# Wide moving operand in the upward matmuls of two MLPs: high and low tokens side by side, two PSUM banks a piece

## What is computed

```python
def rms_norm(x, g):
    xf = x.astype(jnp.float32)
    y = xf * lax.rsqrt(jnp.mean(xf * xf, axis=-1, keepdims=True) + EPS)
    return (y * g.astype(jnp.float32)).astype(x.dtype)

def sq_relu_mlp(h, w_up, w_down):          # w_up 1024 x 4096, w_down 4096 x 1024
    return jnp.square(jax.nn.relu(h @ w_up)) @ w_down

for layer in range(2):
    x = x + mix(layer, rms_norm(x, norm_mix_g[layer]))
    x = x + sq_relu_mlp(rms_norm(x, norm_mlp_g[layer]), mlp_w_up[layer], mlp_w_down[layer])
```

## Time and profile before

| | us |
|---|---|
| median of 3 runs (lowest, highest) | 897.57 (897.37, 898.06) |
| the profiled execution | 897.22 |
| its span, from first to last instruction | 895.4 |
| TensorE busy in the span | 887.2 (99%) |
| VectorE busy | 572.0 (64%) |
| ScalarE busy | 466.5 (52%) |
| DMA: mean rate | 184 GB/s |

### The profile page before, as it was taken

One profiled execution on the slowest core, in us unless ns is written; L12 is line 12 of the kernel. 1 busy time (PEld: TensorE's weight loads), 2 busy tenths in 40 slices (PEclk: granted clock), 3 DMA queues, 4 the chain that ended last, 5 costly groups with the idle time before them and its releaser, 6 DMA issues.

```text
span 895.4 us, 14765 instructions
## 1 busy us (share of the span) xinstructions
PE 887.2 (99%) x5978; PEld 787.2 (88%) x5978; DVE 572.0 (64%) x948; ACT 466.5 (52%) x747; POOL 59.7 (7%) x69
## 2 busy tenths in 40 slices
PE   9999999999999999999999999999999999999998
PEld 5998799999997888669999999878898889999996
DVE  5769675555554395566556565564567798888764
ACT  5686454444443387646555544454367674344550
POOL 0010000000000045400000000031100000000000
PEclk9999999999999999999999999999999999999999
DMA  8625786555545745378555555530535455554541
GB/s 303 256 94 188 272 316 223 202 187 188 188 143 179 280 146 184 131 259 325 187 197 191 183 188 188 188 106 1 188 111 186 143 186 179 181 183 145 184 144 47
DMA packets 30885, 164.99 MB, mean 184 GB/s; under 512 B 3425, under 2 KB 9953, under 8 KB 12514
## 3 DMA queue, kind: packets, MB, share of 16 engines
q1 hardware_dynamic: 30818, 164.04, 51.6%
HBM read 162.98 MB, written 1.05 MB: 183 GB/s over the span
## 4 chain that ended last, share of the span: by engine, by line
PE 93%; DVE 3%; ACT 1%; DMA 1%; issue 1%; POOL 0%; DVEq 0%; SPq 0%; POOLq 0%; ACTq 0%
PE ps L283 15%; PE ps L285 15%; PE ps L284 15%; PE ps L296 11%; PE ps L297 11%; PE ps L298 11%; PE ps L424 2%; PE ps L361 1%; PE ps L926 1%; PE ps L925 1%; PE ps L924 1%; DMA BI<-in_dbias_dram 1%; DVE WL L1592 1%; PE ps L839 1%; PE ps L864 1%
## 5 line engine op out<-in xcount | busy, mean ns | idle before, releaser
L1592 DVE TENSOR_TENSOR WL<-RAW,WH 128x1024 fp32r<-128x1024 f32 (+1 forms) x260 | 307.1, 1218 | 109.9 <-ACT WH L1002 109.5
L283 PE MATMUL ps<-XAh,WH 128*128 128x256 f32 x1152 | 330.1, 287 | 0.0
L285 PE MATMUL ps<-XAh,WL 128*128 128x256 f32 x1152 | 325.9, 283 | 0.0
L284 PE MATMUL ps<-XAl,WH 128*128 128x256 f32 x1152 | 325.9, 283 | 0.0
L1002 ACT CAST WH<-RAW 128x1024 fp32r<-128x1024 f32 (+1 forms) x264 | 262.1, 1044 | 64.7 <-PE ps L298 62.0
L283 PEld LDWEIGHTS ps<-XAh,WH 128*128 128x128 f32 x1152 | 220.8, 192 | 9.1 <-issue 6.6
L284 PEld LDWEIGHTS ps<-XAl,WH 128*128 128x128 f32 x1152 | 220.8, 192 | 1.8 <-issue 0.7
L285 PEld LDWEIGHTS ps<-XAh,WL 128*128 128x128 f32 x1152 | 220.8, 192 | 0.0
L296 PE MATMUL ps<-WH,HTh 128*128 128x512 f32 x256 | 99.9, 390 | 0.0
L297 PE MATMUL ps<-WL,HTh 128*128 128x512 f32 x256 | 99.9, 390 | 0.0
L298 PE MATMUL ps<-WH,HTl 128*128 128x512 f32 x256 | 99.6, 389 | 0.0
(11 more groups left out here) (258 smaller groups left out, 1101.5 us busy)
## 6 DMA issues: line engine op xcount, KB each, us to landing
RAW<-in_w_dram SPq DMA_DIRECT2D x141, 1024.0 KB, 5.0
RI<-in_w_dram SPq DMA_DIRECT2D x2, 1024.0 KB, 10.6
GB<-in_gb_dram SPq DMA_DIRECT2D x4, 512.0 KB, 6.7
BI<-in_dbias_dram SPq DMA_DIRECT2D x16, 128.0 KB, 4.7
NB<-in_nbias_dram SPq DMA_DIRECT2D x16, 128.0 KB, 2.6
RAW<-in_w_dram SPq DMA_DIRECT2D x2, 528.0 KB, 3.6
X<-in_x_dram SPq DMA_DIRECT2D x4, 256.0 KB, 3.5
RAW<-in_w_dram SPq DMA_DIRECT2D x2, 512.0 KB, 6.6
```

The lines of the kernel that those rows point to most:

```text
L283: T.e.matmul(dst, h, xh[:, k, :], start=k == 0, stop=False)
L284: T.e.matmul(dst, h, xl[:, k, :], start=False, stop=False)
L285: last = T.e.matmul(dst, l, xh[:, k, :], start=False, stop=k == 7)
L1592: D.e.tensor_tensor(M.WL[:, c.s, sl], M.RAW[:, c.r, sl], M.WH[:, c.s, sl].bitcast(F32), ALU.subtract).then_inc(*S.lo.tick(key, a))
```

## The change

- The two XA tiles become halves of one tile X2 (128 x 8 x 512): for each k, 256 high token columns and 256 low ones side by side.
- A new routine `columns_wide` makes the upward pieces 2 to 15 of both MLPs. For each m and k there are two matmuls: high weights by all 512 columns of X2, into a whole bank, and low weights by the 256 high columns, into that bank's first half. So a piece takes two banks: even pieces 4 and 5, odd ones 6 and 7.
- ScalarE copies the second halves of the two banks into RL, without relu; VectorE adds the first halves from PSUM (new semaphore `up`) and then makes max(r, 0) * r into SQ. Pieces 0 and 1 keep the old way out, and their square takes the new form as well.
- TensorE waits for `up` of piece j-2 where it waited for the relu, at piece 2 for the relu of piece 1, at piece 3 for HTh and HTl of piece 0 (MLP 1: the ada columns too).
- In MLP 1 the context transposes go between upward piece j and downward piece j-2 of the rounds 6 and 10, behind a wait for `up` of j-1; the shift on ScalarE comes right after the copy of the rounds 6 and 10, ahead of the weight casts; pieces 7 and 11 wait for it.
- Later users of banks 4 to 7 wait for `up`.

```diff
--- before.py
+++ after.py
@@ -139,7 +139,9 @@
 
         self.WH = self.tile("WH", [128, NW, 2048], F32R)
         self.WL = self.tile("WL", [128, NW, 2048], F32R)
-        self.XA = self.tile("XAh", [128, 8, 256], F32R), self.tile("XAl", [128, 8, 256], F32R)
+        self.X2 = self.tile("XA", [128, 8, 512], F32R)
+        self.XA = self.X2[:, :, 0:256], self.X2[:, :, 256:512]
         at = self.top
         self.XB = self.tile("XBh", [128, 8, 256], F32R), self.tile("XBl", [128, 8, 256], F32R)
         self.top = at
@@ -226,7 +228,8 @@
         self.top = tmp
         self.CV2 = self.tile("CV2", [128, 2, 512])
         self.YB, self.YC = ([v[:, 4 * z:4 * z + 4, :] for v in self.XB] for z in range(2))
-        self.PS = [stack.enter_context(nc.psum_tensor(f"ps{i}", [128, 512], F32)) for i in range(8)]
+        self.banks = stack.enter_context(nc.psum_tensor("ps", [128, 8, 512], F32))
+        self.PS = [self.banks[:, i, :] for i in range(8)]
         self.stats, self.columns_used = {}, 0
         self.CH = chunks()
         self.ORDER = [key for key, _ in order() if self.CH[key].i is not None]
@@ -283,6 +286,20 @@
             T.e.matmul(dst, h, xh[:, k, :], start=k == 0, stop=False)
             T.e.matmul(dst, h, xl[:, k, :], start=False, stop=False)
             last = T.e.matmul(dst, l, xh[:, k, :], start=False, stop=k == 7)
+    return last
+def columns_wide(T, M, S, key, bank):
+    c = M.CH[key]
+    for m, a in ((0, 0), (0, 1), (1, 0), (1, 1)):
+        T.wait_ge(*S.hi.at(key, a))
+        T.wait_ge(*S.lo.at(key, a))
+        for k in range(4 * a, 4 * a + 4):
+            h, l = weights_of(M, c, k * 256 + m * 128, 128)
+            T.e.matmul(M.PS[bank + m][:, :], h, M.X2[:, k, :], start=k == 0, stop=False)
+            last = T.e.matmul(M.PS[bank + m][:, 0:256], l, M.XA[0][:, k, :], start=False, stop=k == 7)
     return last
 
 
@@ -516,16 +533,28 @@
         T.wait_ge(*S.htl.at(l, j))
 
     for j in range(2, 16):
-        T.wait_ge(*S.relu.at(l, j - 2))
-        columns_matmul(T, M, S, ("up", l, j), M.XA, 4 + j % 2).then_inc(*S.freed.tick("up", l, j))
+        if j == 2:
+            T.wait_ge(*S.relu.at(l, 1))
+        elif j == 3:
+            T.wait_ge(*S.hth.at(l, 0))
+            T.wait_ge(*S.htl.at(l, 0))
+            if l:
+                T.wait_ge(*S.adac.at(2))
+        else:
+            T.wait_ge(*S.up.at(l, j - 2))
+        if l and j in (7, 11):
+            for n in range(2):
+                T.wait_ge(*S.cev.at(j // 4 - 1, n))
+        columns_wide(T, M, S, ("up", l, j), 4 + 2 * (j % 2)).then_inc(*S.freed.tick("up", l, j))
+        if l and j in (6, 10):
+            context_transposes(T, M, S, j // 4 - 1, j)
         hready(j - 2)
         for t, n in TN:
             if j == 2:
                 T.wait_ge(*S.res.at("dsa" if l else "rec", t, n))
             made = rows_group(T, M, S, ("down", l, j - 2), hidden(j - 2), 0, t, n, j == 2, False)
         made.then_inc(*S.freed.tick("down", l, j - 2))
-        if l and j in (5, 9):
-            context_transposes(T, M, S, j // 4 - 1)
 
     for t in range(2):
         for n in range(2):
@@ -538,14 +567,11 @@
                     made.then_inc(*S.acc.tick(f"mlp{l}", t, n))
 
 
-def context_transposes(T, M, S, t):
+def context_transposes(T, M, S, t, j):
+    T.wait_ge(*S.up.at(1, j - 1))
     for n in range(2):
         T.wait_ge(*S.cxn.at(t, n))
-        if t == 0:
-            T.wait_ge(*(S.htl.at(1, 0) if n else S.adac.at(2)))
-        else:
-            T.wait_ge(*S.cev.at(0, n))
         for q in range(4):
             at = n * 512 + q * 128
             made = T.e.transpose(M.PS[6 + n][:, q * 128:(q + 1) * 128], M.CX[:, at:at + 128], M.cc("id", 0, 128))
@@ -559,8 +585,7 @@
 
 def tensor_dsa(T, M, S):
     k = 2
-    T.wait_ge(*S.relu.at(0, 15))
-    T.wait_ge(*S.htl.at(0, 0))
+    T.wait_ge(*S.up.at(0, 15))
     ada_matmul(T, M, S, 1, 0, 5)
     norm_transposes(T, M, S, k, 0)
     ada_matmul(T, M, S, 1, 1, 5)
@@ -579,7 +604,6 @@
         if not t:
             made.then_inc(*S.kv.tick())
 
-    T.wait_ge(*S.relu.at(0, 14))
     ckv(0, 4)
     norm_transposes(T, M, S, k, 1)
     ada_matmul(T, M, S, 1, 2, 5)
@@ -747,8 +771,7 @@
 
 def tensor_second(T, M, S):
     free = {b: S.res.at("mlp1", b // 2, b % 2) for b in range(4)}
-    free[4], free[5] = S.relu.at(1, 14), S.relu.at(1, 15)
-    free[6], free[7] = S.cev.at(1, 0), S.cev.at(1, 1)
+    free[4], free[5], free[6], free[7] = S.up.at(1, 14), S.up.at(1, 14), S.up.at(1, 15), S.up.at(1, 15)
 
     def take(b):
         T.wait_ge(*free[b])
@@ -1139,14 +1162,17 @@
     def relu(j):
         A.wait_ge(*S.freed.at("up", l, j))
         if j >= 2:
-            A.wait_ge(*S.htl.at(l, j - 2))
-        elif j == 0:
+            A.wait_ge(*S.sq.at(l, j - 2))
+            b = 4 + 2 * (j % 2)
+            A.e.copy(M.RL[:, j % 2, :].rearrange("p (m q) -> p m q", m=2), M.banks[:, b:b + 2, 256:512]).then_inc(*S.relu.tick(l, j))
+            return
+        if j == 0:
 
             if l:
                 A.wait_ge(*S.pv.at(7))
             else:
                 A.wait_ge(*S.ybl.at(3))
-        A.e.activation(M.RL[:, j % 2, :], M.PS[4 + j % 2 if j else 4][:, :], AF.Relu).then_inc(*S.relu.tick(l, j))
+        A.e.activation(M.RL[:, j, :], M.PS[4 + j][:, :], AF.Relu).then_inc(*S.relu.tick(l, j))
 
     def hth(j):
         if j:
@@ -1180,6 +1206,8 @@
     high(A, M, S, "down", l, 1)
     for j in range(2, 16):
         relu(j)
+        if l and j in (6, 10):
+            context_shift(j // 4 - 1)
         if j < 14:
             high(A, M, S, "up", l, j + 2)
         if j == 14:
@@ -1187,8 +1215,6 @@
         hth(j)
         if l and j in (4, 8):
             context_squares(j // 4 - 1)
-        if l and j in (6, 10):
-            context_shift(j // 4 - 1)
         if j < 14:
             high(A, M, S, "down", l, j)
         if j == 14:
@@ -1827,9 +1853,14 @@
         D.wait_ge(*S.relu.at(l, j))
         if j >= 2:
             D.wait_ge(*S.hth.at(l, j - 2))
+            b = 4 + 2 * (j % 2)
+            r = M.RL[:, j % 2, :].rearrange("p (m q) -> p m q", m=2)
+            D.e.tensor_tensor(r, M.banks[:, b:b + 2, 0:256], r, ALU.add).then_inc(*S.up.tick(l, j))
+            D.wait_ge(*S.up.at(l, j))
         elif j == 0 and l == 0:
             D.wait_ge(*S.ybh.at(3))
-        D.e.tensor_tensor(M.SQ[:, j % 2, :], M.RL[:, j % 2, :], M.RL[:, j % 2, :], ALU.mult).then_inc(*S.sq.tick(l, j))
+        D.e.scalar_tensor_tensor(out=M.SQ[:, j % 2, :], in0=M.RL[:, j % 2, :], scalar=0.0, in1=M.RL[:, j % 2, :],
+                                 op0=ALU.max, op1=ALU.mult).then_inc(*S.sq.tick(l, j))
 
     def hidden_low(j):
         D.wait_ge(*S.hth.at(l, j))
@@ -2647,6 +2678,7 @@
     S.arow = count("arow", [0, 1, 2])
     hidden = [(l, j) for l in layers for j in range(16)]
     S.relu, S.hth = count("relu", hidden), count("hth", hidden)
+    S.up = count("up", [(l, j) for l, j in hidden if j > 1])
     S.cev, S.fev = count("cev", TN), count("fev", TN)
     S.kc, S.qiev = count("keys", range(2)), count("queries", range(2))
     S.kiev = then(S.kc, range(2))
```

## The result

| | before | changed | ratio, 95% interval |
|---|---|---|---|
| median of 7 runs each, us | 897.78 | 894.45 | 0.9958 (0.9947 to 0.9968) |
| the same pair in a second comparison | 898.19 | 893.66 | 0.9952 (0.9939 to 0.9966) |
| span of the profiled execution | 895.4 | 893.0 | |

The time fell by 3.3 us, and by 4.5 in the second comparison. 892.1 was forecast from 897.57, 5.5 us less. The size is that of rival (a), 895.1: its loops were to give 3.0 - 0.5 = 2.5 us, and they gave 2.6. The rest came from outside the loops.

What follows compares the result with a forecast made beforehand. TensorE's spacing of matmul starts was taken to bound the MLP loops. 897.22 profiled - 5.97 (pair) + 0.5 (wait at piece 2) = 891.75; the median is 0.35 above: 892.1 us, range 891.0 to 896.0.

Steps and rivals of the forecast that it cites:

- rival (a): Upward pieces: each wide and narrow pair pays part of the size switch, 0.0067 us; 895.1 us in all; chance 0.13.
- wrong if the pair is not 0.347: Sign set beforehand: TensorE steps inside a late upward piece should take 0.347 us, else the prediction is wrong.
- The pair: Upward pieces 2 to 15, both MLPs: three 256-column matmuls become one of 512 and one of 256; 5.97 us saved.
- I take no surcharge: Upward pieces: surcharge and refund of adjacent size switches were taken to offset each other, leaving 0.3467 us a step.
- The middle value: Upward pieces: a pair pays a third of the first step's surcharge, 0.0067 us; 3.0 us saved.
- The fixed part: TensorE in the MLP loops: each matmul costs 0.0133 us beyond its columns, which dropping 448 matmuls saves.
- Rival (b): MLP loops: the apparent 13.3 ns per matmul mostly comes from unlike neighbours; about 1.1 us saved, 897.0 us; chance 0.08.
- whatever its size: TensorE: the 0.0133 us beyond the columns was claimed for every matmul width, from a line through 256 and 512 columns.
- The wait at piece 2: TensorE waits until ScalarE has read piece 1 from bank 5: 0.5 us stall in MLP 0, nothing in MLP 1.
- The way out: ScalarE copy, VectorE add and new square after upward pieces: some 22 us more VectorE work, hidden, costing nothing.
- The context tiles: MLP 1: moved transposes, shift and second tile's DMA cost nothing, with slacks of 2.4 us and 6 us.
- The gain should reach the end: After the MLPs: a chain through TensorE starts earlier by as much as the loops save, so the whole gain arrives.

Runs made afterwards that it cites:

- runs of 16: Changed kernel with all 16 wide matmuls of a piece first, then its 16 narrow ones: 890.66 us beside 898.52 of the kernel before, ratio 0.9912.
- 2 and 2: Changed kernel with two wide, then two narrow matmuls by turns: 890.95 us, run once.
- 4 and 4: Changed kernel with four wide, then four narrow matmuls in each group of four contraction steps: 893.06 us, run once.

## Why the prediction was right and wrong

The range held the time, and the direction was right. But by its own sign ("wrong if the pair is not 0.347") the prediction was wrong about its main term: the pair took 0.353. The loops alone would have given 897.57 - 2.6 = 895.0, which is inside the range because the range was drawn to hold rival (a). That the measured 894.45 lies nearer to the forecast than this is luck: it comes from a stretch that was not in the sum.

- **The pair**, forecast 5.97 us: pieces of 5.64 instead of 5.75, 26 x 0.112 and 0.19 in the two first pieces, 3.1 us. The step that failed is "I take no surcharge". The surcharge after a change of size was in the rows (0.70 and 0.69), and I let its refund on the way back cancel it. In strict alternation the wide matmul keeps paying 6 to 14 ns and the narrow one returns 0 to 7. The middle value, 0.0067 a pair, would have been right (0.0058 over a piece, 0.0066 inside): rival (a). My reason against it, that the surcharge belongs to a run's start, should have counted for it: in this change every wide matmul starts a run.
- **The fixed part** of 13.3 ns is real for both sizes: in runs of 16 the starts are 0.2263 and 0.120 again. Rival (b) is refuted at its root. The Trainium skill ("TensorE: Matmul & The Clock Gate", section "Wait — 56ns, not 53.3ns?") has 2.5 ns for this term; in these matmuls, each with a weight load of its own, it is 13.3. But "whatever its size" is wrong: at 128 columns the weight load sets the distance (0.112).
- **The wait at piece 2**, forecast 0.5: idle 0.49 in MLP 0, none in MLP 1.
- **The way out**: hidden, as forecast. The square in its new form costs what the old one did (691 ns in both kernels, where up to 0.75 us was allowed), and VectorE's busy time rose by 17.5 us, not 20 to 24. In MLP 0, between 124 and 269 us, TensorE is busy 145.00 of 145.00.
- **The context tiles**: the numbers came close to those worked out. Rows of ScalarE, TensorE and SP's waits in the changed kernel, the end of piece 6 at 461.97:

```profile
462.65 2.91 ACT L1228 ACTIVATE TB<-ps,ADA,AB 128x128 f32<-128x128 f32 x8
...
468.30 0.39 PE L301 MATMUL ps<-XA,WH 128*128 128x512 f32 x1
...
469.56 2.00 ACT L1025 CAST WH<-RAW 128x1024 fp32r<-128x1024 f32 x2 [3.99 <-DMA RAW<-in_w_dram]
...
SPq L127 <- PE ps L577: 18.3, 1, 18.3
```

  The shift ends at T + 3.6 (3.9 was worked out), before piece 7 at T + 6.3. The cast for piece 8 waits 3.99 us for its weights and starts at T + 7.6; piece 8 starts on time all the same. SP's wait grew from 13.2 to 18.3, where 18.8 was worked out. ScalarE has a new stall of 4 us that costs nothing, since TensorE wanted those weights 6 us after they were split. TensorE's only wait inside the loops is the one at piece 2.
- **The sum**: 3.1 - 0.5 = 2.6 us from the loops. "The gain should reach the end" held, and more arrived than the loops gave: the attention part added about 1 us in most profiles, none in the first.

## What to carry to other kernels

Price a matmul by the distance between starts, and for each pair of neighbours: a long one after a short one may cost more than after its like, so group matmuls of one size (here 16 and 16; 2 and 2 was as good, 4 and 4 wasn't). Where the trace shows a surcharge once a run, reckon with it at every step if the change turns every step into a run. Put a wait ahead of the first instruction that needs it, not ahead of the piece.

## What was not expected of the hardware

- Alternating 512 and 256 columns costs 353 ns a pair where runs of each cost 347; runs of two cost less than runs of four.
- With weight loads of 128 columns the starts in a run stay 112 ns apart, with 128 moving columns as with eight; a single 128-column matmul after a wide one starts its successor after 58 ns, and the successor then holds TensorE 280 to 292 ns instead of 227.
- A faster loop goes with other waits for transfers in a stage behind it whose code is the same: bias waits of 5.8 to 6.0 us in total became 4.1 to 5.3.
